# A merge stage with six seven-product pairs, and U's pairs from unit 40 with their token quarters summed in the query stage

## The reference

```python
h = rmsnorm(x, g_mix)
q, k, v, f, gb, gc_in, xc, g_attn, g_conv = split(h @ w_in)
attn = forgetting_attention(q, k, v, f + b_f)         # 8 heads x 64
conv = gb * causal_depthwise_conv3(gc_in * xc)        # 512 channels
y = sigmoid(g_attn) * (attn @ W_a) + sigmoid(g_conv) * (conv @ W_c)   # g_*: 1024 channels each
x = x + y @ w_out
h = rmsnorm(x, g_ffn)
x = x + peer(h)            # 8 heads pick 16 of 128*128 one-neuron experts: sum gate * gelu(h . u_e) * v_e
x = x + sigmoid(rmsnorm(x, g_ple) @ w_pg) * (p @ w_pp)
return rmsnorm(x, g_final)
```

## Time and profile before

| | |
|---|---|
| median of three runs | 1727.42 us |
| time of the profiled execution | 1726.77 us |
| its span on the core | 1725.0 us |
| TensorE busy | 1718.0 us |
| VectorE, GpSimd, ScalarE busy | 1338.5, 979.1, 724.8 us |
| start of the merge stage's second chunk | 201.81 us |
| U's first pair | 704.07 us |
| end of the pairs | 1107.42 us |

### The profile page before, as it was taken

How to read it: one execution, slowest core, us unless ns; L and a number is a source line. 1 busy time by engine, 2 the same in 40 slices (tenths; PEclk the granted TensorE clock), 3 DMA queues, 4 the chain that set the end, 5 groups by cost and what they waited for, 6 DMA issues and landing times.

```text
span 1725.0 us, 25962 instructions
## 1 busy us (share of the span) xinstructions
PE 1718.0 (100%) x9432; PEld 1495.4 (87%) x9432; DVE 1338.5 (78%) x2424; ACT 724.8 (42%) x1120; POOL 979.1 (57%) x743
## 2 busy tenths in 40 slices
PE   9999999999999999999999999999999999999998
PEld 7888888888888888999999999988888888888887
DVE  7666322468799998999999999656888888888874
ACT  7644322443332222434334333454444444444364
POOL 6333344443347787778877787636666756674100
PEclk9999999999999999999999999999999999999999
DMA  6322332358764443355544464779999999999821
GB/s 215 104 66 71 109 123 95 113 181 313 256 229 150 146 147 112 119 171 155 163 151 161 159 158 156 203 279 334 375 381 375 367 378 371 370 365 381 289 85 50
DMA packets 161759, 363.37 MB, mean 211 GB/s; under 512 B 37056, under 2 KB 78016, under 8 KB 161504
## 3 DMA queue, kind: packets, MB, share of 16 engines
q1 hardware_dynamic: 102224, 259.56, 43.8%
q0 software_dynamic: 40192, 67.41, 11.7%
q10 hardware_dynamic: 19216, 34.74, 5.5%
HBM read 300.54 MB, written 61.01 MB: 210 GB/s over the span
## 4 chain that ended last, share of the span: by engine, by line
PE 96%; DVE 2%; ACT 1%; issue 1%; DMA 0%; POOL 0%; DVEq 0%; SPq 0%; ACTq 0%; POOLq 0%
PE pair L699 18%; PE pair L701 18%; PE pair L700 18%; PE pair L944 15%; PE pair L968 8%; PE pair L967 8%; PE pair L966 8%; PE pair L820 1%; PE pair L908 1%; PE pair L811 0%; PE pair L1051 0%; PE pair L842 0%; POOL wl L619 0%; PE pair L843 0%; DVE rstd L1639 0%
## 5 line engine op out<-in xcount | busy, mean ns | idle before, releaser
L651 POOL DMA_INDIRECT gates<-gate_val,gate_at x336 | 392.2, 1167 | 122.0 <-issue 96.4
L619 POOL TENSOR_TENSOR wl<-raw,wh 128x1024 fp32r<-128x1024 f32 x85 | 205.6, 2427 | 285.8 <-ACT wh L1154 275.8
L1154 ACT ACTIVATE wh<-raw 128x1024 fp32r<-128x1024 f32 x258 | 271.1, 1055 | 119.7 <-PE pair L701 101.2
L699 PE MATMUL pair<-wh,act_h 128*128 128x512 f32 x768 | 299.0, 389 | 0.0
L701 PE MATMUL pair<-wh,act_l 128*128 128x512 f32 x768 | 298.8, 389 | 0.0
L700 PE MATMUL pair<-wl,act_h 128*128 128x512 f32 x768 | 298.8, 389 | 0.0
L672 POOL DMA_INDIRECT picked<-score_dram,score_at x128 | 152.9, 1194 | 145.2 <-PE pair L701 100.8
L1832 DVE TENSOR_TENSOR wl<-raw,wh 128x1024 fp32r<-128x1024 f32 x174 | 211.1, 1217 | 21.1 <-ACT wh L1154 20.5
L679 POOL DMA_INDIRECT rows<-stream,row_at x128 | 141.5, 1105 | 72.0 <-issue 34.7
L699 PE MATMUL pair<-hh,wh 128*128 128x512 f32 x456 | 182.1, 399 | 0.0
L967 PE MATMUL pair<-tl,wh 128*128 128x256 f32 x640 | 181.1, 283 | 0.0
(11 more groups left out here) (309 smaller groups left out, 3774.4 us busy)
## 6 DMA issues: line engine op xcount, KB each, us to landing
raw<-stream SPq DMA_DIRECT2D x337, 512.0 KB, 4.1
score_dram<-gout ACTq DMA_DIRECT2D x128, 256.0 KB, 2.3
gates<-zeros SPq DMA_DIRECT2D x48, 512.0 KB, 6.1
score_in<-score_dram SPq DMA_DIRECT2D x128, 192.0 KB, 6.5
gate<-gates SPq DMA_DIRECT2D x128, 192.0 KB, 6.9
gates<-gate_val,gate_at POOLq DMA_INDIRECT x384
x<-xT SPq DMA_DIRECT2D x7, 512.0 KB, 4.6
picked<-score_dram,score_at POOLq DMA_INDIRECT x128, 5.9
```

Source lines behind the costliest of these rows:

```text
L619: nc.gpsimd.tensor_tensor(wl[:, slot(n), :], raw[:, n % RAW, :], wh[:, slot(n), :].bitcast(F32), ALU.subtract).then_inc(lo_done, 1)
L651: nc.gpsimd.indirect_dma_start(gate_list, at, gate_val[:, r, k:k + 1], None).then_inc(scattered[r], 16)
L699: nc.tensor.matmul(out, ah, bh, start=start, stop=False)
L1154: nc.scalar.activation(wh[:, slot(n), :], raw[:, n % RAW, :], ACT.Copy).then_inc(hi_done, 1)
```

## The change

1. **Merge stage.** Chunks 0 and 1 stay. For chunks 2 to 7 (`MERGE_FROM`, six of them, `M_N`) the units g_attn and g_conv of a chunk are a pair: `merge_products` replaces two `project`s. The products go to banks 0 to 3, the branch units to banks 4 to 7. VectorE joins the products in `sig` (`join`), ScalarE takes both sigmoids from there in one operation of 128x1024, and VectorE merges as before. The weight blocks of two pairs lie in 3.5 slots each; the branch unit's halves have the half slots left (`ATTN_AT`, `CONV_AT`), GpSimd makes their low parts in two operations of 128x512 and none of the pairs'.
2. **The merge stage's token sums** are made once, on VectorE between heads 6 and 7 and behind head 7. Their high parts (`merge_th`) lie in the memory of `x`, one low part over `hl`. `x` is therefore loaded when the last pair's products are done: its four loads move on SP's queue behind the load of unit `U_OUT + 3`.
3. **U.** The pairs begin at unit 40, and there are 42. The token sums of U are made in steps: T1, T2, T3 on VectorE behind the top 16 of query units 2 to 10 and 13 (`token_step`), T4 at the end of the routing's first tile, two low parts at the end of the second; ScalarE's high parts beside them. The fourteen operations before the first pair are gone. The fourth exponential moves to unit 37, and `pace` starts to count in pairs at scatter 114 in place of 128. The candidates' buffer has 12 rows in place of 16, to make room.

The counters of pairs in all waits start with the six merge pairs (`M_N + p`). The diff, cut to its core:

```diff
-PLAIN_SCATTERS = 128
+PLAIN_SCATTERS = 114
-EXP_AT = (5, 16, 28, 38)
+EXP_AT = (5, 16, 28, 37)
-PAIR_U = 44
-PAIR_N = 40
+PAIR_U = 40
+PAIR_N = 42
+MERGE_FROM = 2
+M_N = DC - MERGE_FROM
...
 SP
-                for i in range(DC // 2):
-                    if n == U_MERGE + RAW + SL + 2 + 2 * i:
-                        if i == 0:
-                            sp.wait_ge(logits_ready, 2 * TT * PAIRS)
-                        load_x(i)
+                if n == U_OUT + RAW:
+                    sp.wait_ge(unit_used, U_OUT - 1)
+                    for i in range(DC // 2):
+                        load_x(i)
...
 TensorE
+            def merge_products(m):
+                n, base = U_PAIRED + 3 * m, 4 * (m % 2) * UW
+                low_at, high_at = slice(0, THALF), slice(THALF, T)
+                pe.wait_ge(pair_lo, 4 * m + 1)
+                if m == 0:
+                    pe.wait_ge(mg_out, 1)
+                else:
+                    pe.wait_ge(part_kept, m)
+                quarter(base, A11, psum[3][:, low_at], *tokens(0, 0)).then_inc(made, 1)
+                if m >= 1:
+                    pe.wait_ge(part_added, 4 * m)
+                quarter(base, A12, psum[0][:, low_at], *tokens(1, 0)).then_inc(made, 1)
+                pe.wait_ge(pair_lo, 4 * m + 2)
+                if m == 0:
+                    pe.wait_ge(th_done, 4)
+                    pe.wait_ge(tl_done, 4)
+                quarter(base, A22, psum[2][:, high_at], merge_th[:, T4], merge_tl[:, 2]).then_inc(made, 1)
+                pe.wait_ge(pair_lo, 4 * m + 3)
+                quarter(base, S1, psum[1][:, low_at], merge_th[:, T1], merge_tl[:, 0]).then_inc(made, 1)
+                quarter(base, S2, psum[0][:, high_at], merge_th[:, T2], merge_tl[:, 1]).then_inc(made, 1)
+                pe.wait_ge(pair_lo, 4 * m + 4)
+                quarter(base, S3, psum[1][:, high_at], merge_th[:, T3], tokens(0, 1)[1]).then_inc(made, 1)
+                quarter(base, S4, psum[2][:, low_at], *tokens(1, 1)).then_inc(unit_used, 2)
+            for m in range(M_N):
+                dc = MERGE_FROM + m
+                merge_products(m)
+                wait_low(pe, U_MERGE + 3 * dc + 2)
+                pe.wait_ge(mg_out, max(2, dc - 1))
+                branches(dc, 4 + 2 * (dc % 2), from_at(ATTN_AT), from_at(CONV_AT))
...
 ScalarE
+            merge_quarter(0); merge_quarter(1)      # high parts of T1, T2
+            sigmoid(0, 0); merge_high(0, 0); sigmoid(0, 1); merge_high(0, 1)
+            merge_quarter(2); merge_quarter(3)
+            sigmoid(1, 0); sigmoid(1, 1); branch_high(MERGE_FROM)
+            merge_high(0, 2); merge_high(0, 3)
+            for m in range(M_N):
+                dc = MERGE_FROM + m
+                if m < M_N - 1:
+                    merge_high(m + 1, 0)
+                    first_kept(m)
+                    for k in range(1, 4):
+                        merge_high(m + 1, k)
+                else:
+                    ...                             # high(U_OUT .. U_OUT + 2) around first_kept(m)
+                act.wait_ge(part_added, 4 * m + 4)
+                both = sig[:, dc % 2].rearrange("p u t -> p (u t)")
+                nc.scalar.activation(both, both, ACT.Sigmoid).then_inc(sig_done, 2)
+                if m < M_N - 1:
+                    branch_high(dc + 1)
...
+            for n in range(U_OUT + 3, U_OUT + SL):  # behind the eight copies of merged to hh
+                high(n)
...
 VectorE
             head_done(HEADS - 2)
+            ...                                     # T1, T2: five operations of 128x1024
             head_done(HEADS - 1)
+            ...                                     # T4, T3 and low parts; merge(0); merge_low(0, 0), (0, 1)
+            dve.wait_ge(unit_used, U_MERGE + 5)
+            merge_token_low(3, merge_b)
+            merge_pair_sums(0)
+            merge_low(0, 2)
+            merge_low(0, 3)
+            for m in range(M_N):
+                merge(MERGE_FROM + m - 1)
+                if m < M_N - 1:
+                    merge_pair_sums(m + 1)          # 4 operations of 128x512
+                    for k in range(4):
+                        merge_low(m + 1, k)
+                join(m)                             # 4 operations
...
             for n in range(N_PQ):
                 best(...)
+                token_step(n)                       # one operation of 128x1024 at n = 2..10, 13
...
+                if r == 0:                          # end of the routing's first tile
+                    dve.wait_ge(zero_out, 16 * ZEROS)
+                    link(nc.vector.tensor_tensor(t4, of_tokens(hh, 1, 0), t2, ALU.subtract))
+                    nc.vector.tensor_tensor(t4, t4, of_tokens(hl, 1, 0), ALU.add).then_inc(t_ready, 1)
+                elif r == 1:
+                    token_low(T2, 3)
+                    token_low(T4, 4)
...
             pair_low(0, 0)
             pair_low(0, 1)
-            ...                                     # T1 to T4 and their low parts: 14 operations
```

More of the change, by code:

```diff
@@ L155, in lows_before @@
 def lows_before(n, by_dve):
[L156 to L159 removed]
+    return sum(low_by_dve(k) == by_dve and not paired(k) and not merge_paired(k) for k in range(n))
+EXP_AT = (5, 16, 28, 37)
 TOP_A = 4
 CANDS = TOP_A * TOPK + (TOPK - TOP_A) * TOP_A
[L164 to L165 removed]
+PAIR_U = 40
+PAIR_N = 42
 PAIR_END = PAIR_U + 2 * PAIR_N
@@ L194, in made_by @@
 def made_by(p, k):
-    return PAIR_U + (PAIR_PARTS - 1) * p + k
+    return (PAIR_PARTS - 1) * (M_N + p) + PAIR_U + k
 def highs_before(n):
-    return sum(not paired(k) for k in range(n))
+    return sum(not paired(k) and not merge_paired(k) for k in range(n))
 def kept_before(u):
@@ L639, in scatter @@
                         whole, part = divmod(beat, 2)
-                        units, parts = whole, whole + 1
+                        units, parts = whole, (PAIR_PARTS - 1) * M_N + whole + 1
                     else:
@@ L860, in _, with quarter, tokens, branches @@
             values(last_g)
-            for dc in range(DC):
+            wh_flat = wh[:].rearrange("p s w -> p (s w)")
+            wl_flat = wl[:].rearrange("p s w -> p (s w)")
+            def quarter(base, block, bank, bh, bl):
+                for c in range(KHALF):
+                    at = base + (block * KHALF + c) * P
+                    ah, al = wh_flat[:, at:at + P], wl_flat[:, at:at + P]
+                    nc.tensor.matmul(bank, ah, bh[:, c, :], start=c == 0, stop=False)
+                    nc.tensor.matmul(bank, ah, bl[:, c, :], start=False, stop=False)
+                    last = nc.tensor.matmul(bank, al, bh[:, c, :], start=False, stop=c == KHALF - 1)
+                return last
+            def tokens(k, j):
+                at = (slice(None), slice(k * KHALF, (k + 1) * KHALF), slice(j * THALF, (j + 1) * THALF))
+                return hh[at], hl[at]
+            def branches(dc, first, attn_part, conv_part):
+                for br, bh, bl, part in ((1, conv_h, conv_l, conv_part), (0, attn_h, attn_l, attn_part)):
+                    if dc == 0 and br == 0:
+                        pe.wait_ge(head_out, HEADS)
+                    for c in range(CC):
+                        last = three(psum[first + br][:], part(wh_flat, c), part(wl_flat, c), bh[:, c, :], bl[:, c, :],
+                                     c == 0, c == CC - 1)
+                last.then_inc(unit_used, 1)
+            def from_at(at):
+                return lambda flat, c: flat[:, at + c * P:at + (c + 1) * P]
+            for dc in range(MERGE_FROM):
                 n, b = U_MERGE + 3 * dc, 4 * (dc % 2)
-                if dc >= 2:
-                    pe.wait_ge(mg_out, dc - 1)
                 if dc >= 1:
@@ L873, in _ @@
                     pe.wait_ge(mix_dve, by_dve(len(MIX)) + 1)
[L874 to L880, removed]
+                at = (n + 2) % SL * UW
@@ L1816, in _ @@
+            merge_low(0, 2)
[7 more added lines that the diff above has]
+                join(m)
+            for c in range(DC - 1):
+                split_merged(c)
+            merge(DC - 1)
             split_merged(DC - 1)
```

390 lines of the change are left out of this document (273 added, 117 removed).

## The result

The changed kernel takes 1717.97 us (median of 4 runs, 1717.70 to 1718.21), the kernel before 1727.74 us beside it (1726.21 to 1728.73): ratio 0.9945, 95% interval 0.9933 to 0.9957. The forecast was 1720.8 us, its range 1719.6 to 1724.8. The profiled executions say 1717.87 us (span 1716.1) after and 1726.77 us (span 1725.0) before, a gain of 8.9 us.

What follows compares the result with a forecast made beforehand. PE's work was taken to set the time; 5.0 us from the merge stage and 1.6 from U made 6.6 off 1726.77, 1720.2 us, plus 0.65 to the median: 1720.8. The range was 1719.6 to 1724.8 us.

Steps and rivals of the forecast that it cites:

- the price of a pair: Merge stage and U: 120 ns for each 256-column matmul, taken from U's old pairs, 84 matmuls and 10.08 us a pair.
- the allowance from the profiled execution to the median: Whole kernel: the median of the runs lies 0.65 us above the profiled execution, raising 1720.2 to 1720.8 us.
- Two projections for a pair in the merge stage: Merge stage: 10.92 us of PE become 10.08, 0.83 us for each of six chunks, 5.0 us gained.
- Rival 4: Merge stage: the pairs run 3% above 120 ns a matmul, giving 1722.6 us; chance 0.04.
- Four plain units for two pairs in U: U: four plain units (21.75 us) go for two more pairs (20.17 us), 1.6 us gained.
- No new wait: Merge, query and U's first pairs: DVE's sums ready before PE needs them, slack about 1 and 2 us; cost 0.
- rival 1: DVE late at the first merge pair or unit 40, costing PE 1 to 4 us once: 1721.8 to 1724.8; chance 0.22.
- POOL in DVE's way: Merge stage: DVE operations wait for POOL's, at most 2.4 us a chunk, DVE 13.8 of 15.7 us; PE unaffected.
- rival 3: Merge stage: POOL's shared port makes DVE miss the chunk; 1.1 us a chunk cancels the gain, 3 gives 1739; chance 0.07.
- The scatters' tail: Behind U's pairs: POOL's last scatter ends 0.1 to 0.6 us later against PE, margin 1.0 us, cost 0 to 0.3.
- rival 2: Scatters' last part stays while PE moves 6.6 us: 1726.4 us, or 1721.3 with a 1.5 us slip; chance 0.07.
- The gain from the projections' slower start after a branch unit: Merge stage: pairs could also win back under 0.1 us per projection start, 0.5 us in all, as upper bound.

Runs made afterwards that it cites:

- Run 11: Changed kernel with early_q (and early_t) 192 bytes further, so early_q and late_q both begin at 128 modulo 256; 1720.27 us, ratio 0.9956.
- run 1: Kernel before with 64 unused bytes ahead of the token sums th and tl; 1723.22 us against 1726.95, ratio 0.9974.
- run 5: Kernel before with 128 unused bytes ahead of the token sums th and tl; 1724.44 us, ratio 0.9981.
- run 9: Kernel before with 192 unused bytes ahead of the token sums, which then begin at 64 modulo 256; 1714.61 us, ratio 0.9928.
- run 6: Changed kernel with U's pairs from unit 44 again: 40 pairs, 128 plain scatters, old places of the exponentials; 1720.39 us, ratio 0.9954.
- run 10: Changed kernel with early_q 128 and late_q 192 bytes further, all U's token sums at 64 modulo 256; 1706.97 us, ratio 0.9879.
- run 12: Changed kernel with U's token sums at 64 modulo 256 and the mix stage's tensors 32 bytes further; 1705.60 us, ratio 0.9872.
- run 7: Changed kernel with the weight rings wh and wl (and raw) 64 bytes further, weights at 192 modulo 256; 1721.69 us, ratio 0.9962.
- run 8: Changed kernel with hh and hl 64 bytes further, at 192 modulo 256, weights at their old remainder; 1717.76 us, ratio 0.9939.
- run 4: Changed kernel with the mix stage's tensors (attn, conv, merge_tl) 32 bytes further, at 192 modulo 256; 1717.13 us, ratio 0.9938.

## Why the prediction was wrong

The step that failed is the price of a pair: "I take 120 ns, since the operands have the same shapes and 84 matmuls per pair". It took the rate of one placement for the rate of the shape. The text weighed only the merge pairs against it, and let U's own pairs, 400 us of the kernel, stand at 10.08 us, though the diff moves the tensors that four of their seven products read, and for three of them (T1, T3 and T2's low part, in early_q) to another remainder. Measured, a pair of U takes 10.02 us: 42 x 0.06 = 2.5 us of gain that is in no term of the sum. Run 11 puts the place back and nothing else, and the pair is at 10.08 and the time at 1720.27 again; runs 1, 5 and 9 give the kernel before the same kind of gain by a pad. Of the 2.8 us between forecast and median these are 2.5. The rest is the allowance from the profiled execution to the median, 0.65 us where 0.10 was measured, and the +0.8 and -0.6 of the table. The range had little room on that side by its own words: 0.5 us and as much again below 1720.8 is 1719.8, not 1719.6.

The rest, by the prediction's own steps:

- **Two projections for a pair in the merge stage, 5.0 us.** Right: 219.15 to 229.23 is 10.08 us for the first pair, and the six chunks take 15.68 us each, 4.98 us in all. The matmuls on merge_tl, at remainder 160, are dearer (123 ns) and those behind them cheaper (117 ns), so that each product takes 1.44 us and the pair comes out at the forecast. Rival 4 (3% above) didn't come.
- **Four plain units for two pairs in U, 1.6 us.** Right: run 6 shows 1.7 us on the timeline with the shorter pairs in it.
- **No new wait; rival 1.** It didn't come. DVE's two low parts of sums start at 219.63 and at 679.18, and its first product of sums is due on PE at 223.5 and 682.4:

```profile
219.63 2.49 DVE L2017 TENSOR_TENSOR wl<-merge_sums,wh 128x1024 fp32r<-128x1024 f32 x2
...
236.36 1.76 DVE L1994 TENSOR_TENSOR merged<-sig 128x512 f32<-128x512 f32 x1
238.04 1.78 DVE L2031 TENSOR_TENSOR merge_sums<-raw 128x512 f32<-128x512 f32 x1
...
679.18 2.48 DVE L2342 TENSOR_TENSOR wl<-sums,wh 128x1024 fp32r<-128x1024 f32 x2
```

  The first of each two ends half way, so the slack is 2.6 us in the merge stage (1 was forecast) and 2.0 us at unit 40 (2.0 forecast).
- **POOL in DVE's way; rival 3.** The mechanism is there and costs nothing. Where POOL converts its two halves,

```profile
236.26 3.01 POOL L667 TENSOR_TENSOR wl<-raw,wh 128x512 fp32r<-128x512 f32 x2 [17.71 <-ACT wh L1455]
```

  DVE's two operations of the same time take 1.76 and 1.78 us instead of 0.69, 2.2 us a chunk; 2.4 was the bound taken, for POOL at 2.4 us a chunk where it takes 3.0. DVE is busy for 74.42 of the 94.09 us, 12.4 us a chunk against 13.8 forecast, and then idle for 1.8 to 2.3 us.
- **The scatters' tail; rival 2.** ACT's copy of unit 124 ends at 1110.44 and PE's unit 126 starts at 1111.49: 1.05 us of margin, as before. It didn't come.

The gain from the projections' slower start after a branch unit, taken as an upper bound of 0.5 us, can't be told from the chunks' 4.98.

What stays open is the mechanism. The distance of the two starts orders the results but isn't all of it: moving operand and weights both at 128 gave 120 ns, both at 192 gave 119. The matmuls just before count as well. In runs 9, 10 and 12 the products on hh behind those at 64 took 1.42 us where the others on hh took 1.44; and in the merge stage runs 7 and 8 show other pitches than the remainders alone would give. Nor was it tried whether the place of the output counts, which in the merge pairs is another than in U's.

## What to carry to other kernels

Where PE sets the end, as here, the start addresses of the matmul operands are part of the price of a matmul: before a rate is carried over to moved or new tensors, compare their remainders modulo 256 bytes with those of the row that it comes from. A change that moves tensors should be measured once more with their old remainders, or its gain is credited to the wrong edit (here 2.5 of 9 us). And a pad of 32 to 192 bytes is a cheap trial: run 9 gained 12 us of 1727 with one unused tensor. The best place differs by the width of the matmul, so try it on the operands of one width at a time, and measure it in the stage that is meant: in run 7 the same remainders gave 113 ns in U's pairs and 118 in the merge pairs.

## What the runs showed of the hardware

The mean pitch of fp32r matmuls back to back, all at a granted clock of 1.00 (the 2.4 GHz level), by the remainders modulo 256 bytes of the starts of moving operand and weights. The 256 columns are those of U's pairs, but for the row of 160:

| moving, weights | 256 columns | 512 columns |
|---|---|---|
| 128, 128 | 120 ns | 227 ns |
| 192, 128 | 118 ns (runs 1, 8) | 229 ns (runs 4, 8, and 7 behind the pairs) |
| 0, 128 | 119 ns (run 5) | not run |
| 64, 128 | 113 ns (runs 9, 10, 12) | not run |
| 160, 128 | 123 ns, the matmul behind it 117 (merge_tl) | 233 ns (attn, conv) |
| 128, 192 | 113 ns (run 7; 118 in the merge pairs) | 233 ns (run 7, and 8 behind the pairs) |
| 192, 192 | 119 ns (run 7) | 228 ns (run 7, xh, 65 matmuls) |

The spread is 6% at 256 columns (without the row of 160) and 3% at 512, and of the places that were run at both widths, the best for 256 columns (128, 192) is among the worst for 512. The page TensorE: Matmul & The Clock Gate of the Trainium skill (Step-by-step: what each phase is for) has two independent read ports of PE, so that the next weights' load takes no bandwidth from the running matmul. The runs show that what one start costs depends on the other: with the weights at 128, moving the moving operand from 128 to 192 takes the 512-column pitch from 227 to 229 ns; with the weights at 192 it is 233 ns for a moving operand at 128 (hh) and 228 for one at 192 (xh). So the two operands are not independent in time here. The gap that the Trainium skill gives for an isolated warm matmul (TensorE: Matmul & The Clock Gate, Back-to-back issue gap), by its formula 109 ns for 256 columns, was not the mean pitch in any run; 113 is the nearest.
